# Encoder trunk on one core: the input and the memory taken in by features with 1/rms applied behind the projections, and the neighbourhood outputs formed by features

## The reference, cut to what matters

```python
def rms_norm(x, g):
    y = x * lax.rsqrt(jnp.mean(x * x, axis=-1, keepdims=True) + EPS)
    return y * g

def hybrid_mixer(h, w_in, ...):
    proj = h @ w_in                      # split into mLSTM q k v o, gates; neighbourhood q k v; GLA q k v g, a
    qk = silu(dwconv_centred(concat([ml_q, ml_k]), conv_w, conv_b))
    ...                                  # mLSTM heads (6), GLA heads (5), both directions
    s = einsum(q, k) * d ** -0.5 + bias  # neighbourhood attention, 5 heads of 64
    p = softmax(where(in_win, s, -inf))
    o = einsum(p, v)
    mixed = concat([ml_out, na_out, gla_out])
    return mixed @ w_out

for l in range(2):
    h = h + hybrid_mixer(rms_norm(h, mix_norm_g[l]), ...)
    h = h + memory_cross_attention(rms_norm(h, xattn_norm_g[l]), rms_norm(mem, mem_norm_g[l]), ...)
    h = h + conv_ffn(rms_norm(h, ffn_norm_g[l]), ...)
return rms_norm(h, final_norm_g)
```

## Time and profile before

| | |
|---|---|
| median of 3 runs | 880.57 us (878.48 to 882.46) |
| profiled execution | 878.24 us, span 876.3 us |
| TensorE busy | 861.8 us, 98% |
| VectorE busy | 596.0 us, 68% |
| ScalarE busy | 496.1 us, 57% |
| GpSimd busy | 14.3 us, 2% |
| granted TensorE clock | 0.998 (mean) |
| chain that ended last | TensorE 92%, ScalarE 3%, VectorE 3%, issue 1% |
| DMA | 146.78 MB, mean 168 GB/s |

### The profile page before, as it was taken

The page is one execution under the profiler, slowest core; times in us unless marked ns, Lnnn a source line. Parts: engine busy times, 40 slices in busy tenths (PEclk is TensorE's granted clock), DMA queues, the critical chain, the costliest instruction groups (busy, mean ns, idle before and its releaser), DMA issues.

```text
span 876.3 us, 14948 instructions
## 1 busy us (share of the span) xinstructions
PE 861.8 (98%) x6338; PEld 798.1 (91%) x6338; DVE 596.0 (68%) x820; ACT 496.1 (57%) x689; POOL 14.3 (2%) x35
## 2 busy tenths in 40 slices
PE   8999999999999999999999999999999899999997
PEld 8999998889889999999999999988898899999996
DVE  6887678757657666666577885887665666656655
ACT  7954663658647445445567546745755645445444
POOL 5000000000000000000000000000000000000000
PEclk9999999999999999999999999999999999999999
DMA  9735452364255555555448254335435365555541
GB/s 329 201 102 177 156 178 103 112 226 144 97 193 190 195 190 195 192 191 194 145 140 257 72 171 165 127 115 192 135 109 191 127 212 190 193 196 190 192 169 48
DMA packets 114665, 146.78 MB, mean 168 GB/s; under 512 B 10600, under 2 KB 94760, under 8 KB 114600
## 3 DMA queue, kind: packets, MB, share of 16 engines
q1 hardware_dynamic: 114456, 145.57, 49.7%
q10 hardware_dynamic: 144, 0.26, 0.1%
HBM read 144.77 MB, written 1.05 MB: 166 GB/s over the span
## 4 chain that ended last, share of the span: by engine, by line
PE 92%; ACT 3%; DVE 3%; issue 1%; DMA 0%; ACTq 0%; DVEq 0%
PE bank L665 26%; PE bank L666 25%; PE bank L667 25%; PE bank L706 4%; PE bank L743 2%; PE bank L832 2%; DVE wlo L1455 2%; PE bank L1017 2%; ACT whi L1096 1%; ACT yhi L1119 1%; PE bank L872 1%; PE bank L762 1%; PE bank L849 1%; DVE ylo L1710 1%; PE bank L882 1%
## 5 line engine op out<-in xcount | busy, mean ns | idle before, releaser
L1455 DVE TENSOR_TENSOR wlo<-raw,whi 128x2048 fp32r<-128x2048 f32 (+3 forms) x144 | 306.2, 2133 | 106.1 <-ACT whi L1096 105.2
L1096 ACT ACTIVATE whi<-raw 128x2048 fp32r<-128x2048 f32 (+3 forms) x144 | 257.4, 1793 | 53.5 <-PE bank L667 48.4
L665 PE MATMUL bank<-yhi,whi 128*128 128x256 f32 x704 | 195.1, 277 | 0.5 <-DVE ylo L1471 0.5
L666 PE MATMUL bank<-ylo,whi 128*128 128x256 f32 x704 | 194.6, 276 | 0.0
L667 PE MATMUL bank<-yhi,wlo 128*128 128x256 f32 x704 | 194.6, 276 | 0.0
L665 PEld LDWEIGHTS bank<-yhi,whi 128*128 128x128 f32 x704 | 132.2, 188 | 1.6 <-issue 0.7
L666 PEld LDWEIGHTS bank<-ylo,whi 128*128 128x128 f32 x704 | 132.2, 188 | 0.8
L667 PEld LDWEIGHTS bank<-yhi,wlo 128*128 128x128 f32 x704 | 132.2, 188 | 0.0
L665 PE MATMUL bank<-xhi,whi 128*128 128x256 f32 x320 | 91.4, 286 | 2.2 <-DVE wlo L1455 1.2
L665 PE MATMUL bank<-whi,xhi 128*128 128x512 f32 (+2 forms) x256 | 90.1, 352 | 0.0
L667 PE MATMUL bank<-xhi,wlo 128*128 128x256 f32 x320 | 88.9, 278 | 0.0
(11 more groups left out here) (268 smaller groups left out, 1373.1 us busy)
## 6 DMA issues: line engine op xcount, KB each, us to landing
raw<-in_w_up SPq DMA_DIRECT2D x44, 1024.0 KB, 5.0
raw<-in_w_down SPq DMA_DIRECT2D x22, 1024.0 KB, 4.8
raw<-in_w_in SPq DMA_DIRECT2D x10, 1024.0 KB, 7.3
raw<-in_w_xk SPq DMA_DIRECT2D x8, 1024.0 KB, 5.1
raw<-in_w_xv SPq DMA_DIRECT2D x8, 1024.0 KB, 4.9
raw<-in_w_out SPq DMA_DIRECT2D x8, 1024.0 KB, 4.8
raw<-in_w_xq SPq DMA_DIRECT2D x8, 1024.0 KB, 5.7
raw<-in_w_xo SPq DMA_DIRECT2D x8, 1024.0 KB, 4.9
```

Of the source, the lines that this page charges most:

```text
L665: mm(o, s_hi, m_hi, start=first, stop=False, skip_group_check=True)
L666: mm(o, s_hi, m_lo, start=False, stop=False, skip_group_check=True)
L1096: A(weight(whi, gu), raw[:, gu % RING, 0:SIZE[gu]], ACT.Copy).then_inc(hi_done, 1)
L1455: tt(weight(wlo, gu), raw[:, gu % RING, 0:SIZE[gu]], weight(whi, gu), ALU.subtract).then_inc(lo_done, 1)
```

## The change

Layer 0's input: the host lays out x and mem turned as well (`x_turned`, `mem_turned`). The features of x come in four DMAs of 256 KB into `xT`, and their halves are made with the gain alone. The factor 1/rms is applied where each projection leaves PSUM: as a scale per partition where tokens are on partitions, and as a product with `xr`, a row of 1/rms spread over all partitions by a small product (`rx`), where features are. `gq`, `mix` and `qk0` are loaded and split in halves (`HALVED`); `nqk4` comes ahead of `qk0`; x by tokens is loaded behind `qk1`. The mem is multiplied by its own row (`rm`). `keep_clock` has 6 products in place of 12. GpSimd doesn't wait for the input, and makes its masks in another order. Both layers: probabilities are scaled by `shares_of` before they are turned; `nao` has three groups of products (pairs of heads (0, 1), (2, 3), and 4) that give the outputs by features, as the next projection wants them; `yna_hi` and `yna_lo` take them, and they are no longer turned. `wo0` begins with block k = 3. The drains in `layer_drains` follow.

```diff
-    for i in range(4):
-        job(f"n1_{i}", 2 + i)
     if l:
+        for i in range(4):
+            job(f"n1_{i}", 2 + i)
...
+NA_OUT = (3, 5, 6)
+NA_PAIRS = ((0, 1), (2, 3), (4,))
+NA_K = range(3, 6)
...
@@ sync
+                if name == "qk2" and l == 0:
+                    for t in range(TT):
+                        sp.dma_start(h[:, t, :], a["x"][t * P:(t + 1) * P, :]).then_inc(tok_in[t], 16)
+                    sp.dma_start(pcols[:, 0, KT:], a["params"][:, 0, KT:]).then_inc(prm_in[0], 16)
...
@@ tensor
-            keep_clock(12, ps[BANK[0, "qk0"]])
+            keep_clock(6, ps[BANK[0, "qk0"]])
...
+                else:
+                    fm_unit("nqk4", "n1")
+                    fm_blocks("qk0", "n1", [(0, 0, KT), (1, 0, 4)])
+                    pe.wait_ge(root_in, 1)
+                    free("rx")
+                    for t in range(TT):
+                        last = mm(bank("rx")[:, t * P:(t + 1) * P], r1[:, t, 0:1].broadcast_to([P, P]), ident[:], start=True, stop=True)
+                    last.then_inc(te_done, 1)
+                    fm_blocks("qk0", "n1", [(1, 4, KT)])
+                    fm_blocks("qk1", "n1", [(0, 0, 4)])
...
                 for hh in range(NAH + 2):
+                    if hh in NA_OUT:
+                        p = NA_OUT.index(hh)
+                        is_drained(pe, l, f"nat{NA_PAIRS[p][-1]}")
+                        free(f"nao{p}")
+                        for jt in range(TT):
+                            for g in NA_PAIRS[p]:
+                                r = slice(64 * (g % 2), 64 * (g % 2) + 64)
+                                last = mm(bank(f"nao{p}")[r, 0:T], nav[:, jt, g * DH:(g + 1) * DH], npt[:, g % 2, jt].rearrange("p a b -> p (a b)"),
+                                          start=jt == 0, stop=jt == 1, skip_group_check=True)
+                        last.then_inc(te_done, 1)
                     if 1 <= hh <= NAH:
                         g = hh - 1
-                        pe.wait_ge(np_ready, NAH * l + g + 1)
+                        pe.wait_ge(npn_ready, NAH * l + g + 1)
...
                     for k in (i, i + 4):
+                        if k not in MIXED_K:
+                            continue
...
@@ scalar, layer 0
+                    hi_half("gq", 0)
+                    act.wait_ge(gain_in, 16)
+                    input_hi(range(2))
+                    hi_half("gq", 1)
+                    input_hi(range(2, KT))
+                    hi_half("mix", 0)
+                    hi_half("mix", 1)
+                    split_hi("nqk4")
+                    hi_half("qk0", 0)
+                    hi_half("qk0", 1)
+                    split_hi("qk1")
+                    for t in range(TT):
+                        act.wait_ge(tok_in[t], 16)
+                        square_all(h, t)
...
+                    act.wait_ge(mix_scaled, 1)
+                    b = mix_part
...
-                split_hi("qk1")
+                split_hi("qk1" if l else "qk2")
                 conv(0)
...
+                else:
+                    act.wait_ge(mem_in, 16 * TT)
+                    for t in range(TT):
+                        square_all(mtm, t)
...
@@ vector, layer 0
+                    split_lo("qk1")
                     for t in range(TT):
+                        root_ready(t)
+                        link(V.reciprocal(r1[:, t, 0:1], rt[:, t:t + 1]))
+                    ts(r1[:, :, 1], r1[:, :, 0], 0.5, None, ALU.mult).then_inc(root_in, 1)
+                    is_filled(dve, l, "rx")
+                    drain(V.tensor_copy(xr, bank("rx")[:, 0:T]))
+                    is_drained(dve, l, "rx")
+                    is_filled(dve, l, "mix")
+                    tt(mix_part, bank("mix")[:, 0:T], xr, ALU.mult).then_inc(mix_scaled, 1)
...
+                def scaled_qk(i):
+                    is_filled(dve, l, f"qk{i}")
+                    tt(qe[:, 2 * i:2 * i + 2, :], bank(f"qk{i}", 2, T), xr_for(2), ALU.mult).then_inc(scaled_ready, 1)
...
                     split_lo(ahead[hh])
+                    if l == 0 and ML_FILL[hh][0] in SCALED:
+                        scaled_block(ML_FILL[hh][0])
+                    if l == 0 and hh == 3:
+                        dve.wait_ge(mem_turned_in, 16)
+                        is_drained(dve, l, "rm")
+                        tt(memT[:], memT[:], mr.rearrange("p (o n) -> p o n", o=1).broadcast_to([P, KT, T]), ALU.mult).then_inc(memn_ready, 1)
...
+                def shares_of(g):
+                    dve.wait_ge(np_ready, NAH * l + g + 1)
+                    link(V.reciprocal(nsum[:, 2 * g:2 * g + 2], nsum[:, 2 * g:2 * g + 2]))
+                    for t in range(TT):
+                        last = ts(np_[:, g % 2, t, :], np_[:, g % 2, t, :], nsum[:, 2 * g + t:2 * g + t + 1], None, ALU.mult)
+                    last.then_inc(npn_ready, 1)
+
+                def heads_lo(p):
+                    dve.wait_ge(na_hi_ready, 3 * l + p + 1)
+                    r = slice(0, 64 * len(NA_PAIRS[p]))
+                    drain(tt(forwards(yna_lo[r, p, :]), backwards(bank(f"nao{p}")[r, 0:T]), forwards(yna_hi[r, p, :]), ALU.subtract))
...
                     if hh == 0:
                         split_lo("ggb")
+                        for g in NA_PAIRS[0]:
+                            shares_of(g)
...
                         if l == 0:
                             split_lo("xk2")
+                        for g in NA_PAIRS[1]:
+                            shares_of(g)
...
                             split_lo("xk3")
+                        heads_lo(0)
...
                     if hh == 4:
                         split_lo("xv0a")
-                    if hh == 5 and l:
-                        head_squares(mlh, sq, 0, MLH)
+                        shares_of(4)
+                    if hh == 5:
+                        if l:
+                            head_squares(mlh, sq, 0, MLH)
+                        heads_lo(1)
...
-                for k in range(KT):
+                for k in MIXED_K:
```

379 lines of the change are left out of this document (244 added, 135 removed).

## The result

The changed kernel takes 893.25 us (median of 4 runs, 892.54 to 894.39); the kernel before, run beside it, 879.64 (878.48 to 882.46). The ratio is 1.0152, with a 95% interval of 1.0131 to 1.0174: 13.6 us slower, where 3.7 were forecast, and outside the range. In the comparisons that follow, the kernel before had medians of 878.2 to 879.7 us.

A forecast was written before the change was run, and what follows sets the result against it. The prediction took TensorE's own instruction stream, busy 98% of the span, as the bound. Its terms +1.0 (start and mLSTM), +1.2, +3.0 (neighbourhood layers 0, 1) and -1.5 (mixed outputs) gave +3.7 on 880.57: 884.3 us, range 880 to 889.

The forecast's parts named there:

- the landing of the transfers at the start: Layer 0: at the earlier kernel's DMA rate `qk1` lands at 15.0 us and x at 17.5; bounds 1 earlier to 2 later.
- the place of `nv`'s split in VectorE's queue: mLSTM stage, layer 0: a wait of only 0.13 us was forecast at `nva`.
- first scores: Layer 0: TensorE's first scores (`mls0`) start at 48.8 us, against 50.29 before.
- scores to `nas`: Layer 0, from first scores to neighbourhood scores: `nas` at 100.3 us against 99.25, after scores at 48.8 against 50.29.
- `nas` to `kt0`, layer 0: Neighbourhood stage, layer 0: TensorE waits 1.95 us for head 4's scaling; +1.2 us after 1.55 saved.
- `nas` to `kt0`, layer 1: Neighbourhood stage, layer 1: TensorE waits 4.4 us for head 2's scaling and 0.8 at head 4; `kt0` +3.0 us.
- The start: Layer 0: TensorE could reach the scores 5.2 us early, but ScalarE's and VectorE's chains leave 0.4 us at `nq`.
- The mLSTM stage: Layer 0: VectorE's added scalings cost waits of 1.4 us in all; the stage ends 1.0 us later than before.
- The neighbourhood stages: Both layers: paired outputs save TensorE 1.55 us a layer, but turning waits for VectorE's scaling: +1.2 and +3.0 us.
- The mixed outputs: Both layers: four of 16 turnings and a wait of 0.32 us go; -0.76 us a layer, -1.5 in all.
- rival (b): Gaps at the scores and in layer 1 halve TensorE's clock behind them: +3 us together, 887.3 us; chance 0.22.
- Rival (a): Whole kernel: everything is covered and TensorE stays the bound, -9.8 us, 870.8 us; chance 0.12.

The follow-up runs named there:

- e12: Input half with e6's queue order, roots taken early from the turned rows (other numbers), their spreading 24 products earlier: 882.26 us, 1.0037 to the kernel before.
- e6: Input half alone (e1) with two VectorE scalings, of the third pair and of the gate keys, moved forward in its queue: 884.99 us, 1.0059.
- e5: Changed kernel with small throwaway products in six TensorE gaps, about half as many as in e3: 889.74 us, 1.0116 to the kernel before.
- the last of the experiments: VectorE's third-pair scaling moved behind the split of the value weights' second half: in e15 (giving e17, 1.0033) and in e16 (giving e18, 1.0032).
- e17: e15 with VectorE's third-pair scaling moved behind the split of the value weights' second half: 881.62 us, 1.0033 to the kernel before.
- e3: Changed kernel with small throwaway products of the identity in six TensorE gaps, which they outlasted: 899.53 us, 1.0240 to the kernel before.
- e7: Input half alone (e1) with the spreading of the roots (`rx`) 12 products later in TensorE's order: 888.21 us, 1.0092 to the kernel before.
- e15: e6 with `z` 12 products forward on TensorE and the memory's squares and roots behind the first mLSTM head: 885.16 us, 1.0060.
- e1: Kernel before with the input and memory half of the change alone: 888.07 us, 1.0098.
- e2: Kernel before with the neighbourhood half alone (heads' outputs by features, scaled probabilities, mixed outputs): 885.77 us, 1.0069.
- e14: e6 without ScalarE's squares and roots of the memory's rows, memory scaled by the input's 1/rms: 883.03 us, 1.0046 to the kernel before.
- e18: e16 with VectorE's third-pair scaling moved as in e17: 881.40 us, 1.0032 to the kernel before.
- e13: e12 with VectorE's split of the second pair's weights behind the spread roots' copy and the scaling of the gates' parts: 882.55 us, 1.0041.
- e4: Neighbourhood half alone (e2) with VectorE's scalings of probabilities moved forward in its queue: 881.42 us, 1.0022 to the kernel before.
- e10: Neighbourhood half alone (e2) with nothing but VectorE's order changed, in both layers: 876.95 us, 0.9973 to the kernel before.
- e11: The whole change with the moves of e6, e7 and e10 joined: 884.06 us, 1.0054 to the kernel before.
- e16: The whole change as in e11 with the two moves of e15 added: 882.33 us, 1.0034 to the kernel before.

## Why the prediction was wrong, step by step

The steps that failed are three: the landing of the transfers at the start, the place of `nv`'s split in VectorE's queue, and the half clock behind gaps, which the sum did not contain. The terms beside the two traces:

| | forecast, us | traces, us |
|---|---|---|
| first scores | -1.5 | +2.8 |
| scores to `nas` | +2.5 | +8.2 |
| `nas` to `kt0`, layer 0 | +1.2 | +1.5 |
| `nas` to `kt0`, layer 1 | +3.0 | +5.5 |
| the rest | -1.5 | -1.9 |
| sum | +3.7 | +16.1 (medians 13.6) |

**The start: right in kind, wrong in size.** "TensorE's first product at 5.6", it was 7.00; the roots at 19.7 were there at 23.0, the parts of `mix` taken at 25.53 and not 21.8. The length behind it held: 27.0 us forecast from the take to the scores, 27.6 measured. The failed term is the landing: I let everything come in at the rate of the kernel before. These rows (KB each, median us from issue to landing) answer:

```profile
tmb<-in_x_turned SPq DMA_DIRECT2D x4, 256.0 KB, 5.0
h<-in_x SPq DMA_DIRECT2D x2, 512.0 KB, 7.8
raw<-in_w_in SPq DMA_DIRECT2D x4, 1024.0 KB, 8.8
```

I gave that term -1 to +2 us. Measured by when ScalarE could use a unit, `nqk4` was 1.3 us late, `qk0` 1.6, `qk1` 2.9 and the second rows of x 4.0. Two things in the traces bear on it. From 3 to 7 us the queues moved 266 GB/s, where the kernel before had 412. And SyncE stood still twice, because the ring of three buffers had no free one until VectorE had made a low half (L1619); so `qk1` was issued at 11.81 us only, with both halves of x right behind it:

```profile
SPq L601 <- DVE wlo L1619: 2.8, 1, 2.8
SPq L590 <- DVE wlo L1619: 2.8, 1, 2.8
```

How much each of these took was not tested. The scores stood 2.8 us behind and not 1.5 before, 4.3 of the difference between forecast and traces. But the landing alone does not explain the time: e12, where the roots did not wait for it, had its scores 0.7 us before the kernel before's and was still at 1.0037, about 1.9 us under e6; what it lost lay behind them, 53.3 us from the scores to `nas` for 49.0.

**The mLSTM stage: 2.5 us forecast, 8.2 measured.** The gap ahead of `nq` (1.16 us for 1.1) and the wait at `mlo2` (0.54 for 0.65) were as forecast. `nv` waited 1.68 us for 0.13: I placed VectorE's split of `nv`'s two weight halves (2.9 us) in my sum of busy time but not ahead of the scaling of `gk` in the queue; e6 shows that this place was the cause. Block by block against the kernel before, 1.2 us lie ahead of `nq`, 0.7 at `mlo2`, 2.0 at `nv`, and the other 4.3 are half clock in `nq` and `nv`. The 0.6 us that I had at `gvb` did not come.

**The neighbourhood stages: the mechanism was right.** Layer 0 +1.5 for +1.2, with 1.70 us of wait at head 4 for 1.95. Layer 1 4.15 us at head 2 for 4.4, but +5.5 for +3.0; 1.9 of the difference is half clock, the wait at head 4 was 0.53 for 0.8, and the remaining 0.6 I have not broken down. A pair took 1.0 to 1.2 us from start to start (e5 and the changed kernel) for 0.97.

**The mixed outputs.** Forecast -1.5; the rest of the span lost 1.9 in the two traces. Over the ten traces with the neighbourhood half the rest is 706.0 us on average, over the ten without it 707.7: -1.6, about as forecast, with single traces up to 3 us apart.

**The clock, rival (b).** It had the mechanism and 0.22, and it happened. The premise that the trace before "has no gap above 0.84 us after the first product" was misread: there is one of 1.73 at 686.25 us, with full clock behind it. The price of 3 us was that of two gaps; there were four, and TensorE lost 7.4 us at half clock, though e5 gives back only 3.5 of the time measured. What failed is that I put it beside the sum as an alternative: the sum itself contained gaps of 3 and 4.4 us, and the price should have stood in it. With it the forecast had been 887.3, and with the 4.3 us of the start 891 to 892. The rule of the Trainium skill ("TensorE: Matmul & The Clock Gate", What's actually happening), that the gate follows how busy the engine has been, agrees with the rows: granted 0.66 behind 4.15 us of idleness. It does not tell which of the shorter gaps below cost the clock.

**Rival (a)** did not happen. That TensorE is busy for 98% did not protect it: at the first scores the forecast found 1.5 us of cover, and the traces put ScalarE's and VectorE's chain 4.3 us later than that.

## What to carry to other kernels

When work is taken from the bound engine, measure first how far the others are behind it at the next hand-over: here the forecast itself found 1.5 us for 5.2 that TensorE was to win at the start, and in the trace nothing of it could be kept. Moved scalings cost little where they run and much by the place in the queue where they stand: the same instructions took the neighbourhood half from 1.0069 to 0.9973 by order alone. A forecast gap of 2 us or more is to be priced with the half clock behind it, 1.4 to 2.7 us each in this kernel. And a wait that keeps its length whatever is moved has both its ends counted from one event: look for an engine that works without a gap up to the wait, and for what started that run. At the scores this was VectorE from the third pair's scaling on, and only the last of the experiments used it.

## What the runs showed of the hardware

- Which gaps cost the clock. Behind the first 20 us of a trace, half rate followed every gap of 2 us or more (4.17, 4.15, 3.20, 2.68, 2.52, 2.45, 2.26, 2.16, 2.15 and 2.03 us). In front of the first product gaps of 2.20 (changed kernel) and 2.37 (e17) were followed by full rate; in e3, e7 and e15, with similar gaps, the clock was half from about 8 to 12 us.
- Between 1 and 2 us it falls either way, for equal instructions too. The gap of 1.67 to 1.68 at `nv`, with one of 0.54 ahead of it, was followed by half rate in the changed kernel and e1, and by full rate in e7. Every kernel has a gap of 1.73 or 1.74 us between 685 and 707 us: behind it the clock stayed full in 18 traces and fell in e2 and e5. Here the kernel before, and the window (686 to 692), then e2, and the window (696 to 699):

```profile
686.25 2.21 PE L762 MATMUL bank<-ident,tmb 128*128 128x128 f32 x16 [1.73 <-DVE tmb L1447]
686.00:692.00 6.00, 5.18 (x40) 4.76 (x41) 4.25 (x11) 4.45 (x11) 0.00 (x0) 1.00 0.00 0
```

```profile
694.26 2.88 PE L787 MATMUL bank<-ident,tmb 128*128 128x128 f32 x16 [1.73 <-DVE tmb L1481]
696.00:699.00 3.00, 3.00 (x15) 2.73 (x14) 2.59 (x7) 3.00 (x9) 0.00 (x0) 0.50 0.00 0
```

- Two gaps with the scores' 1.1 us between them: 1.98, 1.73 or 1.67 and then 1.16 (changed kernel, e1, e6, e14) were followed by half rate, 0.61 and 1.16 (e17) and 1.15 and 1.16 (e18) were not. In e13 the clock fell within the scores, behind 1.67 alone. Single gaps of 1.70 (changed kernel, e2), 1.67 and 1.64 (e4) and 1.29 (e5) were followed by full rate. Behind the gap of 1.15 at `kt0` of layer 1 and the small products that follow, the clock fell in e10 and e18 and not in e11 and e16.
- Small products in the gap held the clock at 1.00 in all filled gaps of e3 and e5. One of 128 columns of 4-byte numbers took 0.23 us and left two records.
- In 5 of the 20 traces the clock was also half for some 3 us around 30 us with no gap of TensorE above 0.25 us, behind the eight products of `z` (e2, e4, e15, e17, e18). The same stretch in the kernel before and in e2, whose instructions are the same there (busy us, granted clock, DMA share, GB/s):

```profile
29.00:34.00 5.00, 5.00 (x47) 1.00 0.88 222
```

```profile
29.00:34.00 5.00, 5.00 (x29) 0.66 0.85 209
```

That alone moves one execution by 1.5 us, and the first product came 1.0 us later in e2 than in the kernel before; single traces of this kernel can't be compared closer than that.
